# A two-layer decoder trunk on eight cores: the second MLP matmul also as seven block products

## The reference

```python
def squared_relu_mlp(h, w1, w2):
    a = jax.nn.relu(h @ w1)
    return (a * a) @ w2

def reference(x, ...):
    h = x
    for i in range(2):
        if i == 0:
            h = h + conv_mixers(rms_norm(h, ev_norm_g), ...)
        else:
            h = h + chunked_spatial_gating(rms_norm(h, od_norm_g), ...)
        h = h + squared_relu_mlp(rms_norm(h, mlp_norm_g[i]), mlp_w1[i], mlp_w2[i])
    return rms_norm(h, final_norm_g)
```

## Time and profile before

| | |
|---|---|
| median of 3 runs | 2641.08 us (2637.53 to 3118.6) |
| profiled execution | 2640.4 us, span of its slowest core (6) 2638.0 us |
| spans of the eight cores | 2625.3 to 2638.0 us, granted clock 0.991 to 0.993 |
| TensorE busy | 2552.2 us, 97% |
| VectorE / ScalarE / GpSimd busy | 1397.5 / 1052.1 / 834.5 us |
| DMA | 361.33 MB, mean 137 GB/s |

### The profile page before, as it was taken

The page is one execution under the profiler, slowest core; times in us unless marked ns, Lnnn a source line. Parts: engine busy times, 40 slices in busy tenths (PEclk is TensorE's granted clock), DMA queues, the critical chain, the costliest instruction groups (busy, mean ns, idle before and its releaser), DMA issues.

```text
span 2638.0 us, 40660 instructions; the slowest of 8 cores (2625.3 to 2638.0 us)
## 1 busy us (share of the span) xinstructions
PE 2552.2 (97%) x12952; PEld 1218.5 (46%) x12952; DVE 1397.5 (53%) x2269; ACT 1052.1 (40%) x1792; POOL 834.5 (32%) x1028
## 2 busy tenths in 40 slices
PE   5879999999999999999999999999999999999998
PEld 2434444444454444444454444454445444445443
DVE  4754546654566335664457533564345653357334
ACT  2433245434344226534533423643443433364323
POOL 2225342534313223333411323233431133314323
PEclk9989999999999999999999999999999999999999
DMA  9858894676752223167555223214446333302322
GB/s 193 214 138 200 193 198 120 140 143 139 243 182 100 106 89 120 41 181 190 170 202 176 89 95 130 73 53 164 148 144 216 108 118 115 127 30 106 117 90 80
DMA packets 121904, 361.33 MB, mean 137 GB/s; under 512 B 24416, under 2 KB 70496, under 8 KB 104672
## 3 DMA queue, kind: packets, MB, share of 16 engines
q1 hardware_dynamic: 73536, 230.67, 25.3%
q0 software_dynamic: 37072, 55.58, 14.0%
q10 hardware_dynamic: 11088, 72.49, 7.7%
HBM read 326.20 MB, written 88.08 MB: 157 GB/s over the span
## 4 chain that ended last, share of the span: by engine, by line
PE 87%; DMA 7%; DVE 4%; issue 2%; SPq 1%; ACT 1%; ACTq 0%; DVEq 0%; POOL 0%; POOLq 0%
PE bank L926 34%; PE bank L838 25%; PE bank L779 11%; PE bank L766 8%; DMA scr_s<-Z 4%; PE bank L909 3%; PE bank L605 2%; PE bank L1049 2%; DVE Z L438 2%; DMA Z<-ev_w_in 1%; PE bank L715 1%; DMA scr_a<-Z 1%; PE bank L1288 1%; SPq L1119 1%; DMA Z<-scr_s 0%
## 5 line engine op out<-in xcount | busy, mean ns | idle before, releaser
L926 PE MATMUL bank<-Z 128*128 128x512 bf16 x4096 | 910.3, 379 | 0.0
L438 POOL TENSOR_TENSOR Z<-Z 128x512 bf16<-128x512 f32 x512 | 530.7, 1050 | 737.5 <-ACT Z L823 437.1
L787 DVE TENSOR_TENSOR h<-bank,h 128x512 f32<-128x512 f32 x640 | 431.0, 688 | 489.8 <-PE bank L926 386.2
L926 PEld LDWEIGHTS bank<-Z 128*128 128x128 bf16 x4096 | 399.5, 98 | 475.4
L438 DVE TENSOR_TENSOR Z<-bank,Z 128x512 f32<-128x512 f32 x336 | 232.0, 691 | 481.9 <-PE bank L838 463.9
L838 PE MATMUL bank<-Z 128*128 128x512 f16 x1792 | 429.9, 380 | 9.6 <-DVE Z L438 9.4
L766 PE MATMUL bank<-xnT,Z 128*128 128x512 f16 x1792 | 398.9, 382 | 5.6 <-DVE Z L1152 2.2
L845 ACT ACTIVATE Z<-bank 128x512 f32<-128x512 f32 x336 | 189.6, 589 | 527.9 <-PE bank L838 525.4
L823 ACT ACTIVATE Z<-Z 128x512 f32<-128x512 f32 x336 | 211.3, 630 | 333.0 <-DVE Z L438 332.8
L838 PE MATMUL bank<-xnT,Z 128*128 128x512 f16 x1344 | 327.5, 380 | 0.0
L838 PEld LDWEIGHTS bank<-Z 128*128 128x128 f16 x1792 | 174.6, 98 | 223.8 <-issue 15.1
(11 more groups left out here) (100 smaller groups left out, 1768.9 us busy)
## 6 DMA issues: line engine op xcount, KB each, us to landing
...
Z<-wcache SPq DMA_DIRECT2D x55, 896.0 KB, 4.9
...
wcache<-Z SPq DMA_DIRECT2D x28, 896.0 KB, 8.5
Z<-w POOLq DMA_DIRECT2D x48, 512.0 KB, 6.4
...
h<-x SPq DMA_DIRECT2D x32, 512.0 KB, 10.2
...
```

The lines of the kernel that those rows point to most:

```text
L438: P.op(eng, lambda e: e.tensor_tensor(out=out, in0=in0, in1=in1, op=op), reads=reads, writes=writes)
L787: small("dve", lambda e: e.tensor_tensor(out=h[:, tb, d * 512:(d + 1) * 512], in0=banks[b][:], in1=h[:, tb, d * 512:(d + 1) * 512], op=ALU ...
L926: r = e.matmul(banks[b][:], lhsT=lhs(kc, tb), rhs=where[slot].v[:, kc, :], start=start and x_ == 0, stop=stop and x_ == len(ks) - 1)
```

## The change

In quarters 0 to 2 of every MLP the second matmul is done by seven block products too: tokens halved (`hid` columns), hidden channels halved, output columns halved. The sums of hidden tiles (`hsum`, four VectorE ops per hidden piece m, into `Hs`, with s3 in the place of a21) and the differences of w2 (`prep`, on fresh pieces) are new. `w2` comes as twelve pieces per MLP laid out as the w1 pieces are, plus two plain ones for quarter 3 (`w2z`). `hid` and these weights are float16, the relu scaled by 1/16, and the result by 256. A `W2Job` works on one block of 128 tokens in each half: three of its four result blocks go by a `snap`, a VectorE `via` and a GpSimd add to `h`, the fourth by VectorE from the bank to `h`. The three `snap`s are ScalarE's. w2 of MLP 1 is now fresh in macro tiles 0 and 1. `prep` makes two of its four differences in one instruction of twice the size. The difference of the token halves of the normed activations overwrites a21 in `xnT`. There are seven `rbuf`s in place of ten.

```diff
+RSC = 1.0 / 16
+HSC = 256.0
...
-        Xs = at(NSLOT * 8 * KB, 4, 4, 512, dt=H16)
-        hid = nx(8, T, dt=B16)
-        rbuf = [nx(512) for _ in range(10)]
+        Xs = at(NSLOT * 8 * KB, 3, 4, 512, dt=H16)
+        hid = nx(8, T, dt=H16)
+        Hs = nx(3, 4, 512, dt=H16)
+        rbuf = [nx(512) for _ in range(7)]
...
-                    for d in range(2):
-                        pieces.append((f"w2_{L}", fq * 1024, d * 512))
+                    if fq < 3:
+                        for m in range(4):
+                            pieces.append((f"w2_{L}", fq, m))
+                for d in range(2):
+                    pieces.append((f"w2z_{L}", 0, d * 512))
...
-            return 1 if pieces[i][0] == "w1_1" and n_mt > 1 else 0
+            return 1 if pieces[i][0] in ("w1_1", "w2_1") and n_mt > 1 else 0
...
-            for d, a_, b_ in ((4, 1, 0), (5, 3, 4), (1, 3, 1), (6, 2, 5)):
+            P.op("dve", lambda e: e.tensor_tensor(out=v[:, 0:3:2, :], in0=v[:, 2:5:2, :], in1=v[:, 1:3, :], op=ALU.subtract),
+                 reads=t_.ki(1, 3) + bk(4), writes=bk(0) + bk(2))
+            for d, a_, b_ in ((5, 4, 0), (6, 3, 5)):
                 tt("dve", v[:, d, :], v[:, a_, :], v[:, b_, :], ALU.subtract, bk(a_) + bk(b_), bk(d))
...
-            tt("dve", s3, a11, a21, ALU.subtract, k11 + k21, k3)
+            tt("dve", a21, a11, a21, ALU.subtract, k11 + k21, k21)
...
+        def hsum(m, which):
+            for o_, a_, b_, op in which:
+                (vo, ko), (va, ka), (vb, kb) = hop(o_, m), hop(a_, m), hop(b_, m)
+                tt("dve", vo, va, vb, op, ka + kb, ko)
+
+        SUM_A = (("s1", "a21", "a22", ALU.add), ("s3", "a11", "a21", ALU.subtract))
+        SUM_B = (("s2", "s1", "a11", ALU.subtract), ("s4", "a12", "s2", ALU.subtract))
...
+        class W2Job(Job):
+            wscale = HSC
...
+            def via(self, b0, t_, row, d):
+                P.op("dve", lambda e: e.scalar_tensor_tensor(out=t_.v, in0=banks[b0][:], scalar=HSC, in1=t_.v,
+                                                             op0=ALU.mult, op1=ALU.add), [("ps", b0)] + t_.k(), t_.k())
+                tb = 4 * row + self.cp
+                hv, hk = h[:, tb, d * 512:(d + 1) * 512], [("h", tb, d)]
+                tt("pool", hv, hv, t_.v, ALU.add, hk + t_.k(), hk)
+
+            def last(self):
+                add_to_h(self.c, 4 + self.cp, 1, HSC)
...
+                p, l = prev, w1(fq, 3)
+                l.A()
+                p.C()
+                l.B7()
+                p.D4()
+                if strassen and not (fq == 0 and PLAIN == 2):
+                    sums(1)
+                p.D3()
+                l.B6()
+                if strassen:
+                    ii = [take((f"w2_{L}", fq, m))[0] for m in range(4)]
+                    prep_to(OFF[fq] + 8)
+                    w = [W2Job(ii, c) for c in range(4)]
+                    w[0].M1()
+                    l.D4()
+                    w[1].M1()
+                    sums(2)
+                    l.C()
+                    w[0].M2((0, 1, 2))
+                    l.D3()
+                    sums(3)
+                    w[1].M2((0, 1, 2))
+                    w[0].B7((0, 1, 2))
+                    w[1].B7((0, 1, 2))
+                    w[2].M1()
+                    w[0].M2((3,))
+                    w[1].M2((3,))
+                    w[0].B7((3,))
+                    w[1].B7((3,))
+                    prep_to(OFF[fq] + 9)
+                    w[0].B6()
...
```

More of the change, by code:

```diff
@@ L369, in place @@
             wn, r0, _ = pieces[i]
-            last = wn == "w2_1" and r0 == 3072
+            last = wn == "w2z_1"
             top = LOW if low_only[0] or wn.startswith("ev") or last else NSLOT
-            order = list(range(LOW, top)) + list(range(LOW)) if blocks(i) else list(range(top))
+            order = list(range(top))
             order = [q for q in order if q not in live.values()]
@@ L375, in place @@
                 return None
-            if not blocks(i):
-                order = [q for q in order if q < LOW] or order
+            want = [q for q in order if (q < LOW) == (wn[:2] != "w1")]
+            order = want or order
             q = min(order, key=lambda q: freed[q])
@@ L408, in issue_one @@
                 dst = t_.v
-            P.op("pool", lambda e: e.dma_start(out=dst, in_=src),
-                 reads=[], writes=t_.k(0, n), dma=f"w{q}")
+            P.op("pool", lambda e: e.dma_start(out=dst, in_=src), reads=[],
+                 writes=t_.k(lo, lo + n) if blocks(i) else t_.k(), dma=f"w{q}")
             return True
@@ L840, in go @@
                     return ins
-                P.op("pe", go, reads=keys + t_.ki(wb), writes=[("ps", bank)])
+                P.op("pe", go, reads=keys, writes=[("ps", bank)])
             def snap(self, b):
                 t_ = rb()
-                small("act", lambda e: e.activation(out=t_.v, in_=banks[b][:], func=AF.Copy), [("ps", b)], t_.k())
-                return t_
-            def via(self, b0, t_, row, col):
-                tt("dve", t_.v, banks[b0][:], t_.v, ALU.add, [("ps", b0)] + t_.k(), t_.k())
-                relu_sq(t_.v, t_.k(), t_, row, col)
@@ L865, in B6, with B7 @@
+            def B7(self, ks=(0, 1, 2, 3)):
+                if ks[0] == 0:
+                    self.r = get_bank()
+                self.mm("m7", self.r, ks[0] == 0, ks[-1] == 3, ks)
+                if ks[-1] == 3:
+                    self.s7 = self.snap(self.r)
             def B6(self):
@@ L932, in part, with run, w1 @@
                     used(slot)
+            OFF = [0, 8, 16, 24]
+            def run(job, prev, mid=None):
+                job.A()
+                if prev is not None:
+                    prev.C()
+                if mid is not None:
+                    mid()
+                job.B7()
+                job.B6()
+                if prev is not None:
+                    prev.D4()
+                    prev.D3()
+            def w1(fq, m):
+                i = take((f"w1_{L}", fq, m))[0]
+                prep_to(i - base + 1)
+                return W1Job(i, m)
@@ L934, in mlp, with sums, w2_done @@
+            def sums(m, which=SUM_A + SUM_B):
+                hsum(m, which)
+            def w2_done(fq, c):
+                if pre_mt:
+                    pre_step(pre_mt, fq, 2 * c)
+                    pre_step(pre_mt, fq, 2 * c + 1)
+            prev = None
             for fq in range(4):
+                strassen = fq < 3
                 if fq == 0:
                     plain_part()
-                prev = None
-                for m in range(PLAIN if fq == 0 else 0, 4):
-                    i = take((f"w1_{L}", fq, m))[0]
-                    prep_to(i - base + 1)
-                    job = Job(i, m)
-                    job.A()
-                    if prev is not None:
-                        prev.C()
-                    job.B7()
-                    if m < 3:
-                        job.B6()
-                    if prev is not None:
-                        prev.D4()
-                        prev.D3()
-                    if m == 3:
-                        job.B6()
-                    prev = job
@@ L954, in mlp @@
-                p2 = [take((f"w2_{L}", fq * 1024, d * 512))[0] for d in range(2)]
-                if fq < 3:
-                    post, flush = (lambda tb: pre_step(pre_mt, fq, tb)) if pre_mt else (lambda tb: None), lambda: None
-                else:
-                    post, flush = tail
+                for m in range(PLAIN if fq == 0 else 0, 3):
+                    job = w1(fq, m)
+                    todo = []
+                    if strassen and m > 0:
+                        if fq == 0 and m == PLAIN:
+                            todo = list(range(m))
+                        elif m >= 2:
+                            todo = [m - 2]
+                    run(job, prev, lambda: [sums(q) for q in todo])
+                    if isinstance(prev, W2Job):
+                        w2_done(fq - 1, 3)
+                        if L == 0 and mid_mlp:
+                            mid_mlp.pop()()
+                    prev = job
@@ L959, in mlp @@
+                p2 = [take((f"w2z_{L}", 0, d * 512))[0] for d in range(2)]
+                post, flush = tail
                 head, rest = (0, 1, 4, 5, 2, 6), (3, 7)
```

154 lines of the change are left out of this document (107 added, 47 removed).

## The result

**2769.18 us median** (three runs, 2766.91 to 2771.18) against 2641.08: ratio 1.0493, 95% interval 1.0474 to 1.0512. The change makes the kernel 4.9% slower. The forecast was 2693, with a range of 2615 to 2735, so the time lies 34 us above the range. Comparisons leave runs out in which some cores were granted a lower clock.

What follows compares the result with a forecast made beforehand. TensorE alone was taken to set the time: 2638.0 - 82.9 (matmuls gone) + 112.6 (`D3` waits) + 20 (clock) + 3 (small things) = 2690.7, with 2.4 around the span 2693 us; range 2615 to 2735.

Steps and rivals of the forecast that it cites:

- What goes, -82.9: In 24 W2 phases, seven products of four matmuls replace eight, 112 of 128 matmuls staying: -82.9 us.
- `D3`, +112.6: Job 3's `D3` waits for VectorE's `via` of `C` in every quarter: 38.5 us cached plus 74.1 fresh.
- The interruptions: Each GpSimd op falling among VectorE ops with both inputs in SBUF costs VectorE 0.84 us; `via`s keep their 0.69.
- The clock, +20: TensorE runs half-speed stretches of 3.4 us behind long waits, 15.7 of them losing 1.3 us each: +20 us.
- The two in three: Share of the 10 waits of 2.9 us on TensorE that a half-speed stretch was assumed to follow.
- Small things: Fewer `rbuf`s beside the new DMA issues, and adds to `h` in the tails: 0 to 10 us, taken as +3.
- the sums of `xsum` in place: Differences of `xsum` made in place were said to change no count: 0 us.
- GpSimd +302, VectorE +208: Busy time grows on GpSimd by 24 x 12.6 = 302 us, on VectorE by 24 x 6.4 = 154 plus 9 x 6.
- Rival 1: GpSimd waits for VectorE's runs of sums to end, so `D3` waits are shorter: 2640 us, no change; chance 0.25.
- Rival 2: Savings prevail: `D3` does not wait for VectorE's late `via`, or sums run in empty time: 2558 us; chance 0.12.
- Rival 3: Fresh w2 pieces land late; TensorE waits about 18 us in place of 8.9 in six quarters: 2747 us; chance 0.13.

Runs made afterwards that it cites:

- run 9: Changed kernel with run 1 and edits 4, 5, 6; macro tile 0's second matmul plain, w2 differences formed beside it and stored: 2638.97 us, ratio 1.0001.
- run 1: Changed kernel with `sums(2)` moved behind job 3's `C`: 2716.43 us, ratio 1.0289.
- run 3: Changed kernel with the differences of fresh w2 pieces left out: 2715.8 us, ratio 1.0284.
- run 10: Changed kernel with the burst of fresh w2 differences issued behind job 3's `C`: 2747.15 us, ratio 1.0394.
- Run 2: Changed kernel with the relu's squares on ScalarE in place of GpSimd: 2734.18 and 2736.93 us, ratio 1.0366.
- edit 4: Changed kernel with w2 of MLP 1 formed in macro tile 0 only, then taken from the stored pieces: 2757.82 and 2767.04 us.
- edit 5: Changed kernel with the plain w2 pieces of quarter 3 (w2z) in DRAM as one long run per partition: 2762.99 us, ratio 1.048.
- edit 6: Changed kernel with ScalarE's scaling of the next macro tile's x one step later in MLP 1: 2761.96 and 2778.79 us.

## Why the prediction was wrong

- **What goes, -82.9.** Right. The matmuls are gone, but of the 10.4 us per MLP the cached MLPs of run 9 keep 1.5 to 5; its fifth, 208.7 us with 204.3 busy, has 4.4 of idle where before had 0.7, and some 2 hidden under modelled ends.
- **`D3`, +112.6.** Right in place and cause; in size it measured 99.0, 12% less. The 24 waits come to 35.1 us in the 15 cached quarters (forecast 38.5) and 63.9 in the 9 fresh ones (74.1). Per kind: 1.62 for 1.9, 2.71 for 2.9, 7.54 to 7.70 for 6.9, and 7.5 to 9.3 for 8.9, when the wait of up to 3.8 us on a DMA that stands before it in five of six quarters is counted with it. Runs 1, 3 and 10 show its pieces.
- **The interruptions.** 0.84 us a time is right by the row of 2.45 us for four sums; with four squares among four sums it was 0.70. There I had two squares, so the sums took 1.1 us longer than laid out. That they cost next to nothing is luck: they also began 0.9 us earlier against `D4` than I had them, so its `via` came 0.2 us later than laid out. Run 2 shows the mean.
- **The clock, +20: the failed term that had a row.** Measured 44. I had 15.7 stretches of 3.4 us at 1.3; there are 24, at 1.9 each. Fifteen belong to `D3` and cost 30 us, nine to other waits and cost 15. The two in three was right for waits of 2.7 us (7 of 10). But I carried the 1.3 us a stretch seen behind waits of 2.5 to 3.8 us over to waits of 7 to 9, which cost up to 2.7, and gave the other new waits none.
- **"Small things", +3: the step that failed most.** Idle time in the MLPs grew by 164.6, of which `D3` is 99.0; 65.6 are other waits, and some 15 more are hidden. I laid one stretch out step by step, and took every other place as covered because engines' sums fit. By their releasers, with the 9.6 of before not taken off: `snap` 17.3 (GpSimd's adds hold up ScalarE in the last MLP of a macro tile), w2z 13.7 and w 11.2 (I argued w as a rival, w2z not at all), merged differences 14.4. Of these 8.9 stand at the start of the three fresh MLPs, where the kernel before waited 7.8; 4.26 are new, at `B7` of job 3 in quarter 1 of the first MLP, where VectorE had four sums of 4.67 us ahead of that job's differences. Another 7.3 are five waits of 1.4 to 1.5 us for `xnT` at the start of the cached MLPs, which had none: the sums of `xsum` in place, which I had put at 0, are the ones waited for. The rest, some 10 us, is many waits of up to 0.9 us.
- **GpSimd +302, VectorE +208.** Measured 396 and 338. The adds to `h` at 1290 ns are 69 us of the first difference and the squares at 1097 another 24; the second is in the main the interruptions, which I had in the waits and left out of the busy time: with the squares on ScalarE (run 2) VectorE is busy 153 us less.
- **Rival 1** (VectorE keeps its turn) is refuted by the 4.42 us. **Rival 2** by all 24 waits. **Rival 3** (late weights, 2747) is partly there: its sign, a DMA waited for at the first product of a W2 phase, stands in five of six quarters. Where a piece is late, `D3` waits less in return (2.88 + 6.40, 3.75 + 3.79), so its 9 us per quarter did not come on top. The time above my range is not that rival: it needs the waits that I did not list, and the clock.

By core 0, the measured sum is 2632.4 - 82.9 + 99.0 (`D3`) + 65.6 (other waits) + 44 (clock) + 15 (hidden) - 4.4 (outside the MLPs) = 2769. The step that failed is so the +3 for small things, which measured some 80, and after it the clock's +20, which measured 44.

Still open: the last 4 of the 15 us of hidden time, the worth of edits 4, 5 and 6 alone, whether the `xnT` waits come from the sums' new place (no run changed it), and why the waits of run 9's first MLP are longer than before (12 us on its slowest core, 7 on core 0).
